# Decode attention of a two-layer trunk: softmax per block, four column groups for the scores, factors multiplied in by GpSimd

## The reference, cut to what matters

```python
# A: blocks of 256 past keys; each query keeps the best 3 of the 4 past blocks by q . mean(k)
gate = einsum('bhqd,bhnd->bhqn', q, kmean); _, sel = lax.top_k(gate, 3)
s = where(mask, einsum('bhqd,bhqnkd->bhqnk', q, ks) * scale, NEG_BIG)   # chosen blocks and the own one
o = einsum('bhqnk,bhqnkd->bhqd', softmax(s over n,k), vs)
# B: all keys, with the summed log forget values between key and query added to the score
c = cumsum(logf_all, axis=1)
s = einsum('bhqd,bhkd->bhqk', q, kh) * scale + ct[..., None] - c[:, :, None, :]
o = einsum('bhqk,bhkd->bhqd', softmax(s), vh)
```

## Time and profile before

| | |
|---|---|
| median of 3 runs | 1867.61 us (1861.66 to 1872.43) |
| the profiled execution | 1866.09 us, its span 1864.4 us |
| TensorE, VectorE, ScalarE, GpSimd busy | 1704.0, 1091.5, 637.8, 142.7 us |
| mean granted clock of TensorE | 0.96 |

### The profile page before, as it was taken

The page is one execution under the profiler, slowest core; times in us unless marked ns, Lnnn a source line. Parts: engine busy times, 40 slices in busy tenths (PEclk is TensorE's granted clock), DMA queues, the critical chain, the costliest instruction groups (busy, mean ns, idle before and its releaser), DMA issues. The chain is left out here.

```text
span 1864.4 us, 33407 instructions
## 1 busy us (share of the span) xinstructions
PE 1704.0 (91%) x12457; PEld 1545.8 (83%) x12457; DVE 1091.5 (59%) x1818; ACT 637.8 (34%) x864; POOL 142.7 (8%) x263
## 2 busy tenths in 40 slices
PE   5999999978888789999999999998798886899997
PEld 5999999955565479999999999997555654899996
DVE  6666555466566457666576665545645654766655
ACT  3333332233423324333343333323333333433322
POOL 0000000011122200000000000001023231000000
PEclk9999999989989989999999999998899888999998
DMA  6444455465556534443444445564446565444443
GB/s 183 137 156 149 135 163 135 118 183 156 169 171 204 173 128 161 155 150 132 163 143 156 147 135 159 146 157 133 148 151 208 158 193 148 158 153 140 152 147 112
DMA packets 284168, 287.31 MB, mean 154 GB/s; under 512 B 26542, under 2 KB 272998, under 8 KB 283942
## 3 DMA queue, kind: packets, MB, share of 16 engines
q1 hardware_dynamic: 268290, 239.53, 41.7%
q0 software_dynamic: 14464, 46.48, 7.8%
q10 hardware_dynamic: 1316, 0.03, 0.1%
HBM read 279.59 MB, written 6.40 MB: 153 GB/s over the span
## 5 line engine op out<-in xcount | busy, mean ns | idle before, releaser
L1443 PE MATMUL PS<-xh,whi 128*128 128x320 f32 x1920 | 597.2, 311 | 13.8 <-DVE xl L839 11.2
L1443 PE MATMUL PS<-xh,wlo 128*128 128x320 f32 x1920 | 594.6, 310 | 0.0
L1443 PE MATMUL PS<-xl,whi 128*128 128x320 f32 x1920 | 594.5, 310 | 0.0
L830 DVE TENSOR_TENSOR wlo<-raw,whi 128x2048 fp32r<-128x2048 f32 (+2 forms) x185 | 406.8, 2199 | 265.1 <-ACT whi L577 262.9
L577 ACT ACTIVATE whi<-raw 128x2048 fp32r<-128x2048 f32 (+2 forms) x185 | 340.6, 1841 | 612.4 <-PE PS L1443 604.6
L1443 PEld LDWEIGHTS PS<-xh,whi 128*128 128x128 f32 x1920 | 361.7, 188 | 15.6 <-issue 10.6
L1443 PEld LDWEIGHTS PS<-xh,wlo 128*128 128x128 f32 x1920 | 361.8, 188 | 0.6
L1443 PEld LDWEIGHTS PS<-xl,whi 128*128 128x128 f32 x1920 | 361.7, 188 | 0.0
L1443 PE MATMUL PS<-hh,whi 128*128 128x320 f32 x704 | 217.5, 309 | 0.0
L1443 PE MATMUL PS<-hh,wlo 128*128 128x320 f32 x704 | 217.5, 309 | 0.0
L1443 PE MATMUL PS<-hl,whi 128*128 128x320 f32 x704 | 217.5, 309 | 0.0
(11 more groups left out here) (248 smaller groups left out, 1752.4 us busy)
## 6 DMA issues: line engine op xcount, KB each, us to landing
raw<-in_ffn_w_gate SPq DMA_DIRECT2D x45, 1024.0 KB
raw<-in_ffn_w_up SPq DMA_DIRECT2D x45, 1024.0 KB
raw<-in_ffn_w_down SPq DMA_DIRECT2D x32, 1024.0 KB
raw<-in_w_in SPq DMA_DIRECT2D x64, 512.0 KB
key_pages<-in_cache_moba_k SPq DMA_DIRECT2D x128, 192.0 KB, 2.5
value_pages<-in_cache_moba_v POOLq DMA_DIRECT2D x128, 192.0 KB, 2.9
key_pages<-in_cache_fox_k SPq DMA_DIRECT2D x128, 160.0 KB, 2.6
value_pages<-in_cache_fox_v POOLq DMA_DIRECT2D x128, 160.0 KB, 3.3
```

The lines of the kernel that those rows point to most:

```text
L830: dve.tensor_tensor(wlo[s][:, 0:nk, :], raw[s][:, 0:nk, :], whi[s][:, 0:nk, :].bitcast(F32), ALU.subtract).then_inc(split_done[s], 1)
L1443: last = te.matmul(out, w[wslot][r, kt, cols], x[r, at, :], start=start and n == 0 and m == 0, stop=stop and n == len(ktiles) - 1 and m == 2)
```

## The change

Scores get four column groups: `GROUP_TILES` gives each group two key tiles, one a pair of heads of its own and one shared; the rows become 112, with the last group 16 wide. The past forget sums aren't a matmul any more: the 64 spare columns behind a page's 704 key columns hold five of them (GpSimd's `add_past` writes them), they go through the same transposes, and ones in `qz` (`bsel`) pick them. Each block's exponential runs alone with the block's own maximum (`block_exp`); after the gates a factor for each block and row is formed (`block_factors`), and GpSimd multiplies the weights by it (`scale_weights`) before they are turned. `values` runs in four groups of 128 columns and three of 64.

```diff
-ROWS = NH * DS
+ROWS = 112
+GROUP_TILES = ((1, 0), (2, 0), (3, 5), (4, 5))
+GROUP_ROWS = (32, 32, 32, 16)
+GROUP_PAIR = (128, 256, 384, 512)
+GROUP_REST = ((0, 128), (64, 192), (640, 128))
...
@@ gpsimd
+                def add_past(i):
+                    q, n = divmod(i, NBLK)
+                    if i < 2:
+                        pool.wait_ge(pads_cleared, L + 1)
+                    else:
+                        pool.wait_ge(keys_turned, 3 * (L * BLOCKS + i - 1))
+                    pg = 2 * (n % 2)
+                    pool.tensor_copy(key_pages[:, pg:pg + 2, AW + BW:AW + BW + BH], past_of[:, L, q, 2 * n:2 * n + 2, :]).then_inc(past_in, 1)
...
+                def scale_weights(q):
+                    Q = L * DB + q
+                    if q == 0:
+                        pool.wait_ge(out_tok, (L + 1) * 160)
+                    pool.wait_ge(factors_ready, Q + 1)
+                    pool.wait_ge(weights_ready, (Q + 1) * NBLK)
+                    if Q:
+                        pool.wait_ge(weights_turned, 3 * Q)
+                    for n in range(NBLK):
+                        pool.tensor_scalar(scaled[n], weight_rows[:, 256 * n:256 * n + 256], factors[:, n:n + 1], None, ALU.mult).then_inc(weights_scaled, 1)
+                    pool.wait_ge(new_weights_ready, Q + 1)
+                    pool.tensor_scalar(new_scaled, new_row_all[:, q, :], factors[:, NBLK:NBLK + 1], None, ALU.mult).then_inc(weights_scaled, 1)
+                add_past(0)
+                add_past(1)
+                load_values(0)
+                add_past(2)
+                for i in range(BLOCKS):
+                    q, n = divmod(i, NBLK)
+                    if i + 3 < BLOCKS:
+                        add_past(i + 3)
+                    if n == 0 and q >= 1:
+                        scale_weights(q - 1)
+                    if n == 2 and q >= 1:
+                        load_values(q)
+                scale_weights(DB - 1)
@@ scalar
-                def weights(q):
-                    act.wait_ge(exp_bias_ready, Q + 1)
-                    for n in (0, 2, 1, 3):
-                        act.activation(weight_rows[...], PS[...], ACT.Exp, bias=exp_bias[:, n:n + 1], accum_out=exp_sums[:, n:n + 1]).then_inc(weights_ready, 1)
+                def block_exp(i):
+                    act.wait_ge(block_max_ready, Q * NBLK + n + 1)
+                    if Q:
+                        act.wait_ge(weights_scaled, 5 * (Q - 1) + n + 1)
+                    act.activation(weight_rows[...], PS[...], ACT.Exp, bias=minus_max[:, q, n:n + 1], accum_out=exp_sums[:, q, n:n + 1]).then_inc(weights_ready, 1)
+                def block_factors(q):
+                    act.wait_ge(row_max_ready, Q + 1)
+                    if Q:
+                        act.wait_ge(weights_scaled, 5 * Q)
+                    act.activation(factors[:, :], masked_max[:, :], ACT.Exp, bias=row_stats[:, 0:1]).then_inc(factors_ready, 1)
@@ vector
-                ch.mark(dve.memset(qz[:, :, :, :], 0.0))
-                ch.mark(dve.memset(weight_cols[:, :, ROWS:96], 0.0))
-                ch.mark(dve.tensor_tensor(sel[:, :, :], ...))
...
@@ tensor, block_scores
-                    if n < 2:
-                        if Q:
-                            te.wait_ge(weights_ready, 5 * Q - 3 + 2 * n)
-                    else:
-                        te.wait_ge(block_scores_read, L * BLOCKS + i - 1)
+                    if L * BLOCKS + i >= 2:
+                        te.wait_ge(weights_ready, L * BLOCKS + i - 1)
-                    for g in (1, 2):
-                        te.matmul(o[g], sel[:, q, 32 * g - 32:32 * g], brow[:, 256 * n:256 * n + 256], start=True, stop=False)
                     for m in range(2):
-                        for g in range(3):
-                            last = te.matmul(o[g], qz[:, q, 2 * g + m, :], k[:, 2 * g + m, :, :], start=g == 0 and m == 0, stop=m == 1)
+                        for g, w in enumerate(GROUP_ROWS):
+                            last = te.matmul(o[g], qz[:, q, 2 * g + m, 0:w], k[:, GROUP_TILES[g][m], :, :], start=m == 0, stop=m == 1)
@@ tensor, turn_weights
+                    for u in range(2):
+                        te.wait_ge(weights_scaled, 5 * Q + 2 * u + 2)
+                        for g in range(4):
+                            last = te.transpose(PS[...], scaled[2 * u + g // 2][...], ident[0:ROWS, 0:ROWS])
+                    te.wait_ge(weights_scaled, 5 * Q + 5)
@@ tensor, values
-                        for g, (c, w) in enumerate(GROUPS):
-                            last = te.matmul(o[g], weight_cols[:, pg, 32 * g:32 * g + 32], value_pages[:, pg, c:c + w], ...)
+                        for g, c in enumerate(GROUP_PAIR):
+                            te.matmul(PS[groups[g], bank, 0:128], weight_cols[:, pg, groups[g]], value_pages[:, pg, c:c + 128], ...)
+                        for g, (c, to) in enumerate(GROUP_REST):
+                            last = te.matmul(PS[groups[g], bank, to:to + 64], weight_cols[:, pg, groups[g]], value_pages[:, pg, c:c + 64], ...)
```

More of the change, by code:

```diff
@@ L173, in ring_units @@
             if q >= 1:
-                order += {0: [], 1: [(L, "weights", q - 1, 0), (L, "weights", q - 1, 1)], 2: [(L, "values", q - 1)], 3: [(L, "out", q - 1)]}[n]
+                order += {0: [], 1: [(L, "weights", q - 1, u) for u in range(3)], 2: [(L, "values", q - 1)], 3: [(L, "out", q - 1)]}[n]
             if i == LEVEL0:
@@ L185, in ring_units @@
         q = DB - 1
-        order += [(L, "weights", q, 0), (L, "weights", q, 1), (L, "values", q), (L, "out", q)]
+        order += [(L, "weights", q, u) for u in range(3)] + [(L, "values", q), (L, "out", q)]
     return order
@@ L332, in trunk @@
         out_rows = idle[0:ROWS, 3640:3896]
-        new_weights = idle[0:ROWS, 3896:3960]
+        scaled = [tokp[0:ROWS, n // 2, 768 * (n % 2):768 * (n % 2) + 256] for n in range(NBLK)]
+        new_scaled = toks[0:ROWS, 0:NS]
+        past_of = past[:, :].rearrange("p (l h b g) -> p l b g h", l=DEPTH, h=BH, b=DB)
         newb = weight_rows[0:NS, 0:DB * ROWS].rearrange("p (b c) -> p b c", b=DB)
@@ L798, in _ @@
                         copy_weights(q - 1)
-                weights(DB - 1)
+                block_exp(BLOCKS - 1)
+                block_factors(DB - 1)
                 copy_weights(DB - 1)
@@ L1051, in _ @@
[L1051 to L1055 removed]
+                dve.wait_ge(qf_scaled, L + 1)
@@ L1638, in block_scores @@
                     last.then_inc(block_scores_done, 1)
                 def turn_weights(q):
-                    te.wait_ge(weights_ready, (L * DB + q) * 5 + 5)
-                    bank = ring(L, "weights", q, 0)
-                    for g in range(5):
-                        last = te.transpose(PS[:, bank, ROWS * g:ROWS * g + ROWS], weight_rows[:, 128 * g:128 * g + 128], ident[0:ROWS, 0:ROWS])
-                    last.then_inc(weights_turned, 1)
-                    bank = ring(L, "weights", q, 1)
@@ L1652, in values @@
+                    te.wait_ge(weights_scaled, 5 * Q + 5)
+                    bank = ring(L, "weights", q, 2)
+                    te.transpose(PS[0:NS, bank, 0:ROWS], new_scaled, ident[0:ROWS, 0:ROWS]).then_inc(weights_turned, 1)
                 def values(q):
                     Q = L * DB + q
-                    for u in range(2):
+                    for u in range(3):
                         te.wait_ge(*was_read(L, "weights", q, u))
                     bank = ring(L, "values", q)
-                    o = [PS[32 * g:32 * g + 32, bank, 0:w] for g, (c, w) in enumerate(GROUPS)]
+                    groups = [slice(32 * g, 32 * g + w) for g, w in enumerate(GROUP_ROWS)]
@@ L1663, in values @@
+                        for g, (c, to) in enumerate(GROUP_REST):
+                            last = te.matmul(PS[groups[g], bank, to:to + 64], weight_cols[:, pg, groups[g]], value_pages[:, pg, c:c + 64], start=False, stop=False, skip_group_check=True)
                         last.then_inc(values_used, 1)
-                    p, v = [weight_cols[0:NS, NPG, 32 * g:32 * g + 32] for g in range(3)], toks[0:NS, :]
-                    te.matmul(o[0], p[0], v[:, 384:640], start=False, stop=True, skip_group_check=True)
@@ L1670, in turn_outputs @@
+                    for g, (c, to) in enumerate(GROUP_REST):
+                        last = te.matmul(PS[groups[g], bank, to:to + 64], weight_cols[0:NS, NPG, groups[g]], new_value(c)[:, 0:64], start=False, stop=True, skip_group_check=True)
+                    last.then_inc(value_sums_ready, 1)
                 def turn_outputs(q):
```

211 lines of the change are left out of this document (108 added, 103 removed).

## The result

The changed kernel takes 1849.76 us (median of 4 runs, 1848.90 to 1853.94) against 1870.02 for the kernel before on the same chip: a ratio of 0.991 with a 95% interval of 0.9888 to 0.9932. A second measurement of the same kernel, on another occasion, gave 1855.52 against 1867.01, 0.9938 (0.9917 to 0.996). So it is faster by 11 to 20 us, where a median of 1830, 38 us less, had been forecast.

The account below looks back on a forecast made before the run. TensorE was taken to set the pace of the token mix, with some 43 us idle a layer. Terms 11.0 + 10.9 + 5.8 + 1.6 - 1.1 - 4 - 5 gave 19.2 us a layer, 38 in all: 1830 us, 80% range 1800 to 1862.

Parts of the forecast that it names:

- set-up before the first scores: Before the mix, VectorE's clearing and selector building go, mask copy grows, two additions come: gain 1.6 us a layer.
- first scores to sequence 6's value sums: Loop terms together: scores, first blocks' wait, value sums, weight transposes and growing waits; 22.6 us less a layer.
- 2 x 0.22 = 0.44 us a block ... Left: 11.0: Block scores: four rounds replace six, 14.1 us in 32 blocks, less 3.1 lost in level blocks; 11.0 a layer.
- transposes -1.1: Weight transposes before the value sums: 112 columns in place of 88 and a third bank, costing 1.1 us a layer.
- kept by the level blocks: Blocks running the recurrence's levels, where TensorE waits for VectorE's factors: 3.1 us of scores and 3.6 of waits lost.
- The third rival: Mix's granted clock falls from 0.93 to 0.83, 12 us lost a layer, 1852 us; below 0.83 the mark; chance 0.10.
- First blocks' wait, 10.9: Each sequence's first-block wait for the previous sequence's weights goes: 14.5 us a layer less 3.6 lost among levels, 10.9.
- Value sums, 5.8: Value sums with narrower passes take 3.7 us for 4.52, 0.34 a page: 5.8 us a layer in seven.
- Growing waits, -4: Waits on VectorE and ScalarE grow as TensorE's cover shortens, 3 us, plus 1 for GpSimd: 4 a layer lost.
- The second rival: Chains of small VectorE and ScalarE operations take most of the gain: about 9 us a layer, 1850 us; chance 0.14.
- GpSimd, 0.6 us: One 256-column weight multiplication on GpSimd takes 0.6 us, bounds 0.35 and 0.95; a sequence's five take 2.7.
- the first rival: Slow GpSimd multiplications make the kernel slower: gain gone at 1.54 us each, 1898 us at 2; chance 0.10.
- The tail, -5: Last sequence, uncovered GpSimd: from V, sequence 6's value-sum start, multiplications end V + 21.3, value sums V + 27; costs 5 us.

Follow-up runs that it names:

- before_eight: The kernel before with two more 256-column matmuls a block in column groups 1 and 2, eight score rounds for six: 1885.86 us against 1867.35, 1.0101.
- tail_vector: The changed kernel with the last sequence's five weight multiplications on VectorE instead of GpSimd: 1842.92 us, 0.9867 of the kernel before.
- gpsimd_twice: The changed kernel with each 256-column multiplication on GpSimd made twice, the second waiting for the first: 1914.77 us, 1.0254 of the kernel before.
- tail_all_groups: The changed kernel with the last sequence's multiplications on VectorE and an extra 256-column matmul a block in all four groups: 1833.02 us, 0.9827 of the kernel before.
- tail_warm: As `tail_all_groups`, plus 20 matmuls of 128 columns in the wait before the last weight transposes: 1834.52 us, 0.9825 of the kernel before.

## Why the forecast was wrong

Faster was right, 1830 was not. Point by point, for the records of before and after:

| stretch | forecast, a layer | measured, first and second layer |
|---|---|---|
| set-up before the first scores | -1.6 | -1.6, -1.8 |
| first scores to sequence 6's value sums | -22.6 | -7.8, -16.2 |
| from there to the output matrix | +5 | +6.4, +6.4 |

These add up to -3.0 and -11.6, 14.6 of the 17.2 us between the two spans; the rest lies outside these stretches. The first row, in the first layer, is read between two jobs that both kernels have: 400.81 to 412.11 before, 398.17 to 407.87 after.

```profile
400.81 0.20 PE L1588 MATMUL PS<-K,ncn 5*128 5x5 f32 x1
...
412.11 0.40 PE L1637 MATMUL PS<-keys_t,qz 128*32 128x256 f32 x1
```

```profile
398.17 0.20 PE L1639 MATMUL PS<-K,ncn 5*128 5x5 f32 x1
...
407.87 0.63 PE L1686 MATMUL PS<-keys_t,qz 128*32 128x256 f32 x8
```

**The step that failed: "2 x 0.22 = 0.44 us a block ... Left: 11.0".** The rounds run as forecast (1.00 us a block), and two of them are worth 9.3 us a layer in the kernel before, whose clock hardly moved (`before_eight`). But in the changed kernel they are worth nothing: putting them back costs no time. The step counted a saving of TensorE's work at a fixed clock, and the sum has no term for the clock.

Take the loops from the first to the last scores: they were to be 22.6 us shorter each and are 9.6 and 17.6, so 18 us are missing. In the forecast's terms TensorE's busy time was to fall by 18.8 us (scores 14.1, value sums 5.8, transposes -1.1) and its idle time by 3.8 (the waits' 14.5 less the 3.1 and 3.6 kept by the level blocks and the 4 grown). The idle time fell by 4.3 and 2.4, nearly as forecast. The busy time fell by 5.3 and 15.2: it is short by 13.5 and 3.6 us, and 26 and 1 us more at half rate, at 0.42, are 10.9 and 0.4. In the second record it is short by 14.2 and 9.9, and the clock explains 13.0 and 6.7. So the clock has some 11 of the 18 us missing in the first record, and 20 of the 23 in the second (loops 9.7 and 12.2 shorter). Most of the rest is busy time too, 1 to 3 us a loop, and no run here attributes it.

The third rival had the mechanism, but I gave it 0.10 and looked for a clock of 0.83 as its mark; 0.86 to 0.89 was enough. Its price was also worked out wrong: from 0.93 to 0.83 over 235 us isn't 23 us more at half rate but 2 x 0.10 x 235 = 47, so some 20 us a layer. A fall of 0.05 is what gives its 23 us, and about that was measured.

The Trainium skill, "TensorE: Matmul & The Clock Gate", Part 1, makes the throttled state the default that activity lifts. Here the runs agree: less work a block, and the first loop's clock falls from 0.94 to 0.88, although TensorE's idle time fell too; needless matmuls in, and it is 0.94 again; matmuls in the tail's wait, and the clock behind it is 1.00 in place of 0.50.

**First blocks' wait, 10.9:** right in sum, 9.3 and 10.5 by the two runs that put it back, but only with what the clock does beside it. The idle time alone is 5.1 and 8.2 us with four rounds and 9.3 and 10.5 with six.

**Value sums, 5.8:** right or a little low. A page takes 0.33 us (0.34 forecast), the whole 3.2 to 3.55 us (3.7), 7 to 9 us in seven.

**Growing waits, -4:** not what failed. Products and prompt scores wait 15.9 and 14.4 us where it was 8.1 and 9.5, 6.3 a layer more. The forecast had 3.1 and 3.6 for the level blocks beside these 4, and the idle time as a whole came out near it. The second rival named a growth that took place, but it isn't where the missing us stand.

**GpSimd, 0.6 us:** wrong, 0.99, just beyond my upper bound. On VectorE the mean of the same operation is 0.36 us (`tail_vector`), so GpSimd is 2.8 times slower; by the four in a row, 3.62 against 1.14 us, 3.2 times. The Trainium skill, "GPSIMD Engine Reference", section 3.1 (Elementwise), has 1.96 for an addition of two tensors; the measurement decides. It still hid in the loop but for small waits, with little reserve (`gpsimd_twice`): by the first rival's own sum, 21.8 + 4.4 = 26.2 us of the 27.1 that a sequence has. The first rival's break-even of 1.54 us a multiplication can be held against that run, where one costs 1.94 and a wait: it was 1914.8 against the 1898 reckoned for 2 us, and 15 us of its loops' growth is clock, which that sum left out.

**The tail, -5:** the mechanism was right, its size 6.4. The multiplications end at 650.68, V + 21.9, where V + 21.3 was forecast, and the value sums at V + 28.2 (V + 27). What was missed is that this order was a choice: 7 of these us go with one sequence's multiplications on VectorE.

**Open.** What decides where the clock falls in the loops isn't settled, nor why 256 columns put back raise it and 128 in all groups don't: `tail_all_groups` and `tail_warm` have the same loops, and they took 217.2 and 220.9 us in one record, 224.4 and 228.1 in the other, of which 10 and 1 us more at half rate explain 4 and less than 1. In the tail it is plainer: there what TensorE did in the wait made the difference, in one record of each kernel and in both layers.

## What to carry to other kernels

When work is taken off TensorE in a stretch where it also waits, price the saving twice: at a fixed clock, and with the granted clock of the windows falling. Test it the cheap way: put the same amount of needless matmuls back. If the time doesn't move, compare busy time, idle time and clock: the same busy time with more work is the clock, less idle time is work that lay in waits. Before moving arithmetic to a queue that also issues transfers, ask what stands ahead of it in the last iteration, where nothing covers it, and peel that one off.

## What the runs showed of the hardware

- TensorE's clock took back a whole saving: in one record each, at 0.94 and 0.93 it did in 442.9 us of loops what took 449.1 and 454.4 us with 64 matmuls of 256 columns less in each, at 0.88 and 0.89, and at 0.87 and 0.86. I hadn't expected added matmuls to be free.
- The idle wait of 4.8 us in the tail left the clock at 0.50 behind it; with 20 matmuls of 128 columns in it, the clock behind was 1.00.
- GpSimd: 0.99 us for a multiplication of 112 x 256 float32 by a factor a row, 0.45 for 112 x 64, 0.24 for a copy of 128 x 10; VectorE 0.36 for the first, all by the mean of one.
- Sixteen load issues in a row on GpSimd take 15.8 us (630.79 to 646.62), 1.75 a pair but for the first, and arithmetic behind them waits for all.
- A fourth column group of 16 rows runs beside three of 32: 0.25 us a round with four groups, 0.235 with three, the start included in both.
